# Down projection, three of four inner parts: the weight sum of the seventh product is made by accumulating transfers instead of by VectorE

## The reference

```
def reference(x, mem, positions, ...):
    ...
        hf = rmsnorm(x, norm_ffn[l])
        x = x + (jax.nn.silu(hf @ w_gate[l]) * (hf @ w_up[l])) @ w_down[l]
    return rmsnorm(x, norm_final)
```

## Time and profile before

| | us |
|---|---|
| median of three runs (2799.37 to 2800.37) | 2799.76 |
| the profiled execution, whole | 2800.29 |
| its span in the trace | 2798.1 |
| PE busy | 2731.6 (98%) |
| DVE busy | 1529.4 (55%) |
| ACT busy | 1225.1 (44%) |

### The profile page before, as it was taken

The page is one execution under the profiler, slowest core; times in us unless marked ns, Lnnn a source line. Parts: engine busy times, 40 slices in busy tenths (PEclk is TensorE's granted clock), DMA queues, the critical chain, the costliest instruction groups (busy, mean ns, idle before and its releaser), DMA issues.

```text
span 2798.1 us, 33966 instructions
## 1 busy us (share of the span) xinstructions
PE 2731.6 (98%) x12974; PEld 2262.2 (81%) x12974; DVE 1529.4 (55%) x1894; ACT 1225.1 (44%) x1563; POOL 649.4 (23%) x383
## 2 busy tenths in 40 slices
PE   8999999999999999999899999999999999999997
PEld 7888888788888888877777888888888887788885
DVE  5466665200245200278547666666656567678787
ACT  6444444222245322245446444444444445444445
POOL 6000000344433444312233211211112222121210
PEclk9999999899999999999999999999999999999998
DMA  8332232233332333487338877877787897887964
GB/s 257 99 95 84 68 95 70 72 104 98 94 80 76 91 95 104 116 205 156 98 121 203 177 169 181 192 169 172 175 177 169 179 212 199 212 197 208 182 144 121
DMA packets 373552, 399.99 MB, mean 143 GB/s; under 512 B 28760, under 2 KB 248240, under 8 KB 371376
## 3 DMA queue, kind: packets, MB, share of 16 engines
q1 hardware_dynamic: 307936, 272.07, 31.9%
q0 software_dynamic: 60384, 116.41, 24.6%
q10 hardware_dynamic: 5104, 9.76, 1.1%
HBM read 377.21 MB, written 20.97 MB: 142 GB/s over the span
## 4 chain that ended last, share of the span: by engine, by line
PE 74%; DVE 3%; issue 2%; DMA 1%; ACT 1%; POOL 0%; ACTq 0%; DVEq 0%; POOLq 0%
PE psum L763 15%; PE psum L765 15%; PE psum L764 15%; PE psum L1048 9%; PE psum L1049 9%; PE psum L1050 9%; DMA f_raw<-in_w_down 1%; PE psum L1277 1%; DVE f_lo L2499 0%; ACT f_hi L1761 0%; DMA f_raw<-in_w_up 0%; DMA f_raw<-in_w_out 0%; DVE f_raw L2494 0%; PE psum L992 0%; DVE x_back L2652 0%
## 5 line engine op out<-in xcount | busy, mean ns | idle before, releaser
L2499 DVE TENSOR_TENSOR f_lo<-f_raw,f_hi 128x1024 fp32r<-128x1024 f32 x458 | 559.9, 1224 | 411.1 <-ACT f_hi L1761 410.1
L1761 ACT ACTIVATE f_hi<-f_raw 128x1024 fp32r<-128x1024 f32 x462 | 489.5, 1061 | 652.1 <-PE psum L1050 346.4
L684 POOL TENSOR_TENSOR w_lo<-w_raw,w_hi 128x1024 fp32r<-128x1024 f32 x152 | 371.5, 2458 | 937.0 <-ACT w_hi L1359 916.9
L763 PE MATMUL psum<-op_hi,w_lo 128*128 128x512 f32 x1216 | 486.1, 400 | 0.0
L764 PE MATMUL psum<-op_lo,w_hi 128*128 128x512 f32 x1216 | 474.3, 390 | 0.0
L765 PE MATMUL psum<-op_hi,w_hi 128*128 128x512 f32 x1216 | 474.3, 390 | 0.0
L727 POOL DMA_DIRECT2D f_raw<-in_w_up x132 | 159.5, 1215 | 663.6 <-DVE f_lo L2499 622.2
L1359 ACT ACTIVATE w_hi<-w_raw 128x1024 fp32r<-128x1024 f32 x216 | 224.1, 1055 | 127.4 <-PE psum L765 107.8
L763 PEld LDWEIGHTS psum<-op_hi,w_lo 128*128 128x128 f32 x1216 | 229.0, 188 | 47.8 <-issue 2.6
L765 PEld LDWEIGHTS psum<-op_hi,w_hi 128*128 128x128 f32 x1216 | 228.5, 188 | 48.3
L764 PEld LDWEIGHTS psum<-op_lo,w_hi 128*128 128x128 f32 x1216 | 229.1, 188 | 46.2 <-issue 2.0
(11 more groups left out here) (356 smaller groups left out, 5192.3 us busy)
## 6 DMA issues: line engine op xcount, KB each, us to landing
w_raw<-in_w_in SPq DMA_DIRECT2D x144, 512.0 KB, 4.0
f_raw<-in_w_up POOLq DMA_DIRECT2D x132, 512.0 KB, 6.5
f_raw<-in_w_gate SPq DMA_DIRECT2D x88, 512.0 KB, 3.8
f_raw<-in_w_down SPq DMA_DIRECT2D x66, 512.0 KB, 4.4
f_raw<-in_w_down POOLq DMA_DIRECT2D x66, 512.0 KB, 7.2
f_raw<-in_w_up SPq DMA_DIRECT2D x44, 512.0 KB, 4.8
act_scratch<-c SPq DMA_DIRECT2D x22, 512.0 KB, 6.0
pa_raw<-act_scratch SPq DMA_DIRECT2D x12, 768.0 KB, 8.8
```

What stands on the lines that cost most here:

```text
L684: pool.tensor_tensor(w_lo[:, slot], w_raw[:, slot], w_hi[:, slot].bitcast(F32), ALU.subtract).then_inc(w_lo_ready, 1)
L763: pe.matmul(b[:, 0:n], wl, xh, start=start, stop=False)
L1761: act.activation(f_hi[i % FR][:, :], split_source(i)[:, :], ACT.Copy).then_inc(f_hi_ready, 1)
L2499: dve.tensor_tensor(f_lo[i % FR][:, :], split_source(i)[:, :], f_hi[i % FR][:, :].bitcast(F32), ALU.subtract).then_inc(f_lo_ready, 1)
```

## The change

In parts 1 to 3 the sum for product 6 is no longer made by VectorE. GpSimd issues a fourth accumulating transfer for each (e, c), which adds b21 from memory to the running sum. It comes after the transfers for p = 4 of its part in GpSimd's queue. ScalarE waits for that transfer's semaphore, and the load for product 3 of the next part now waits only until `f_lo` of product 5 has been made. Part 0 stays as it was.

```
-                    for p in ADDS:
+                    for p in ADDS + ((6,) if q else ()):
                         added[3 * e + c] += 1
                         load_of["down", q, p, e, c] = (*(LOW_HOME if p == 4 else SUM_HOME)[e, c], added[3 * e + c])
-                    summed = OUT_SUMS + 4 * NQ + 6 * q + PARTS[q] * e + c + 1
-                    load_of["down", q, 6, e, c] = (*SUM_HOME[e, c], summed)
+                    if q == 0:
+                        summed = OUT_SUMS + 4 * NQ + PARTS[q] * e + c + 1
+                        load_of["down", q, 6, e, c] = (*SUM_HOME[e, c], summed)
...
-                                if freed == 5:
+                                if freed == 5 and q == 0:
                                     sp.wait_ge(f_t_added, load_of["down", q, 6, e, c][2])
                                 else:
                                     sp.wait_ge(f_lo_ready, NO + 28 * NQ + DOWN_AT[q, freed, e, c] + 1)
...
-                last = DOWN_AT[q, {1: 0, 2: 1, 4: 3}[p], e, c]
+                last = DOWN_AT[q, {1: 0, 2: 1, 4: 3, 6: 2}[p], e, c]
...
             for q, m in enumerate(PARTS):
-                for p in ADDS:
+                for p in ADDS + ((6,) if q else ()):
                     for e in range(2):
                         for c in range(m):
                             add_down_block(q, p, e, c)
...
-                    if p == 6:
+                    if p == 6 and q == 0:
                         act.wait_ge(f_t_added, count)
                     else:
-                        act.wait_ge(raw_added[3 * e + c] if p in ADDS else raw_in[x][slot], 16 * count)
+                        act.wait_ge(raw_added[3 * e + c] if p in ADDS + (6,) else raw_in[x][slot], 16 * count)
...
                 if i >= 28 * NQ:
                     q, p, e, c = DOWN[i - 28 * NQ]
+                    if q:
+                        return
                     key = ("down", q, 5, e, c)
```

## The result

The changed kernel takes 2808.83 us (median of six runs, 2806.08 to 2812.07) against 2799.23 us for the kernel before in six runs. The ratio is 1.0036, with a 95% interval of 1.0026 to 1.0046: slower, by about 10 us. That is outside the range of the prediction (2798.0 to 2804.5), and almost on the price of the rival "late loads, slower" (2807.8), which had a chance of 0.13.

The account below looks back on a forecast made before the run. TensorE's stream was taken to bound the kernel. On the profiled clock 2800.29 - 1.32 (sums' gain) + 1.4 (late loads) = 2800.4 us, a median of 2799.8, no change; range 2798.0 to 2804.5.

Parts of the forecast that it names:

- late loads, slower: Rival, product 5 of parts 1 and 2: lateness of plain loads adds up over six chunks; 2807.8 us, chance 0.13.
- the start of product 5's loads: Part 1: first load lands about 2546, under way at 2539.0 behind the rest of an activation block.
- The sums' gain, 1.32 us: Removing VectorE's sums ends TensorE's stall at product 6's second chunk in part 1, 1.32 us; parts 2 and 3 gain 0.
- the 0.9 us gap of part 3: TensorE's gap in part 3, ended by "issue", was said to wait for no VectorE instruction.
- The transfers' work, 17 us for six: Part 1: six new transfers, 2.86 us each of all DMA engines, fit the free room and end about 2562.
- Nothing is late for part 2: The new transfers fit before those for product 1 of part 2 start at 2583.70, which shouldn't be late.
- The pace of product 5's loads, 3.8 us each: Loads sharing with new transfers land 3.8 us apart; the fifth is 0.7 us late, costing 1.4 us over parts 1 and 2.
- the rule: DMA engines go round between queues with work, packet by packet, so plain loads get no precedence over new transfers.
- The 2.9 us to spare: Product 5: of 5.24 us between ScalarE's start and TensorE's chunk, 2.9 us is slack before a late load does harm.
- Part 3, cost 0: In part 3 four new transfers meet four loads, 15 us of work in place of 23, so nothing is lost.
- The freed wait of SyncE: Product 3's loads for the next part are issued some 6 us earlier, behind product 5's in the queue; cost 0.
- The forecast's own sign of being wrong: TensorE waiting over 3 us in product 5 of part 1 or 2 would show the forecast wrong.

Follow-up runs that it names:

- e3: Kernel before, but in parts 1 to 3 neither VectorE nor a transfer adds b21 to product 6's weights; 2796.95 us, ratio 0.9990 to the kernel before.
- e10: Kernel e5 with its change in part 1 only; parts 2 and 3 keep VectorE's sums as in the kernel before; 2798.30 us, ratio 0.9995.
- e5: Changed kernel, but all new transfers of a part are released at once when product 5's first low part is made; 2797.94 us, ratio 0.9994.
- e11: Changed kernel, but SyncE issues the activation block behind product 5's six loads in parts 1 and 2; 2806.44 us, ratio 1.0029 to the kernel before.
- e6: Changed kernel, but in parts 1 and 2 GpSimd issues the new transfers only after the activation block has landed; 2799.00 us, ratio 0.9996.
- e1: Changed kernel, but each new transfer waits until product 5's low part for the same (e, c) has been made; 2798.83 us, ratio 0.9999.
- e4: Changed kernel, but product 3's loads for the next part are issued two chunks later; 2809.47 us, ratio 1.0034 to the kernel before.
- e7: Changed kernel, but the 16 new transfers overwrite the running sum instead of adding to it; 2800.91 us, ratio 1.0002 to the kernel before.

## Why the prediction was wrong

The step that failed is the start of product 5's loads: the forecast had the activation block in front of them as good as through at 2539.0, while in the changed kernel it took turns with the new transfers for over 10 us. The terms in order:

**The sums' gain, 1.32 us: right in place, a little small.** The gap at the second chunk of product 6 went, and parts 2 and 3 gave nothing (e3, e10). It is 1.7 us, above the bound of 1.32: the gap, 0.24 us more at the start of part 2, and somewhat slower matmuls right behind the gap. One reading beside it was wrong, without effect on the sum: the 0.9 us gap of part 3 does wait for VectorE. In every run, before as well, it ends 0.10 us after an addition to the result.

**The transfers' work, 17 us for six: a little high.** The 952 packets of the earlier trace rows didn't quite fill their 10 us. Where q0 had the engines to itself it moved 740 packets in 7 us, so a transfer of 272 is 2.57 us and six are 15 us. The room was there: e5 does the same work in part 1 without a loss. The forecast's end of the six, about 2562, was right (2559.9, which is 2562.3 on the clock of before). "Nothing is late for part 2" held as well.

**The pace of product 5's loads, 3.8 us each: right, but for a reason that wasn't there.** It is 4.0 in e11. The 821 and 823 packets of the earlier trace rows are not one for one: q1 moved nothing until about 2537, and then had the engines nearly alone. That the totals agree is chance, and the 12.2 ns a pair with them. So those rows can't bear what the forecast says of the rule; the rule itself holds where both queues have work, 790 and 786 packets in the changed kernel. With 4.0 in place of 3.8 the forecast's own count would have the fifth load late by 1.5 us, not 0.7.

**The start of product 5's loads: the step that failed.** I had the first load land at about 2546, "under way at 2539.0, behind the rest of an activation block". It landed after 18.3 us, at 2550.7, which is 2553.1 on the clock of before, 7 us later and 3.5 us past the 2549.6 from which on a load does harm. The block was counted with the time it took before. There q0 ran dry at 2538 and the block's 816 small packets had the engines almost alone. With the new transfers queued up q0 never paused, each of those packets took its turn with one of q0's, and the block landed after 14.7 us, where e6 has 6.9; so everything behind it in SyncE's queue started some 8 us later. Even the forecast's 12.2 ns a pair would have shown it: by it 816 packets from about 2537.3 last until 2547.3 and the first load until about 2551, an estimate, 1.5 us past 2549.6. The close spacing of GpSimd's issues had no part in it, since at 1.20 us each from 2531.5 three new transfers were also ahead of the block. e6 shows the cause from one side (no new transfer before the block has landed: no loss in parts 1 and 2) and e11 from the other (the block behind: the weights in time, the block late).

**The 2.9 us to spare: right.** ScalarE began at 2550.80 and TensorE at 2553.26, 2.46 us later, against 5.24 - 2.9 = 2.3 by my count.

**The clock: not in the sum at all.** The gap of 3.5 us cost 2.4 us more in slow matmuls. Part 1's loss of 6.4 us over its floor is 3.66 us for the gap and 2.7 us for longer steps right behind it, 2.4 us of them at the lower clock.

**Part 3, cost 0: wrong,** 2.1 us. Without a block the four loads still landed after 12.0 us instead of 4.5: the first after 10.1 us, and the others 3.3 to 4.0 us apart, where ScalarE wants one every 2.72 us. The forecast compared amounts of work, 15 us against 23, and not when each load would be through. With the same transfers later (e1, e5) part 3 loses nothing.

**The rivals.** "Late loads" had the place, the kind of wait and the size (9.4 us for two parts; measured 4.7 + 4.2 in parts 1 and 2, and 2.1 in part 3, net of the gain). Its chance was too low because I let it depend on the pace, 4.4 us and more, while the pace was met and the block's delay decided. Its mechanism was only half right: the lateness didn't add up from load to load, the first load was already 7 us behind. That its 2807.8 us came so near is in part luck: it was scaled from part 0, and had neither the clock's 2.4 us nor part 3's 2.1. The forecast's own sign of being wrong came too, TensorE waiting over 3 us in product 5 (3.5 us in part 1, 3.3 in part 2). The freed wait of SyncE cost nothing, as said (e4).

What stays open: why a load's first packets come some 3 us after its issue when q0 is full (2.7 us before, 3.6 in the changed kernel); and how much of the addition's price is the adding and how much the number of packets.

## What to carry to other kernels

When work moves from an engine to DMA queues, don't ask only whether its bytes fit in the pauses. Find what any engine issues soon behind the new transfers, and follow the first item, a large block in small packets above all, since all behind it in its queue inherits its delay. Read packet counts over windows short enough to show when each queue was at work. And place the new transfers by need: here a release some 18 us later, behind the urgent loads, took the loss of 10 us away with the same traffic (e1, e5).

## What the runs showed of the hardware

- Alone on the engines q0 moved 740 packets of accumulating transfers in 7 us, 2.57 us for one of 512 KB. Side by side with plain loads of 512 KB, a transfer and a load take 4.0 us (e11, five steps from 2540.0 to 2560.0).
- While both queues had work they moved one packet for one, 790 and 786 in 10 us, though q1's were of 1 KB and q0's of 2 KB. A block of 768 KB in 816 packets went from 6.7 us to 14.7 that way.
- The first packets of a load came 2.7 to 3.7 us after its issue in part 1, with q0 at work (before, changed, e6, e7, e11).
- GpSimd issued four transfers within 3.06 us, 0.73 us apart, though each row of a single issue shows 1.20 us.
- Gaps of TensorE of 3.5 us (changed kernel) and 2.8 us (e11) were followed by a stretch at the lower clock, gaps of 1.0 to 1.4 us in part 2 and of 1.8 us in e11's part 2 were not.
- With a DMA share of 0.99 over 114 us TensorE had no gap (e5), and with 0.94 it lost 6 us: the share tells nothing about lateness.
- A gap that the profile puts down to "issue" can be a wait for an engine: in e1 it ended 0.10 us after VectorE's addition, as the same gap did in the kernel before.
